# Opening of a two-layer encoder kernel: x brought in twice, once with its columns as rows, and two weight tiles of the mixer rounded later

## What is computed

```
x = layer_norm(ALPHA * x + 0.5 * (silu(x @ w_up[:, :2816]) * (x @ w_up[:, 2816:])) @ w_down)   # ffn1
u, q, k, v, qi, ki, wi, g_ssm, g_attn = split(x @ w_in)
y_ssm  = state_space(u); y_attn = sparse_attention(q, k, v, qi, ki, wi, rel_bias)
merged = sigmoid(g_ssm) * (y_ssm @ w_branch[0]) + sigmoid(g_attn) * (y_attn @ w_branch[1])
x = layer_norm(ALPHA * x + merged @ w_out)                                                       # mixer
x = layer_norm(ALPHA * x + 0.5 * swiglu(x, ffn2_w_up) @ ffn2_w_down)                             # ffn2
```

## Time and profile before

| what | us |
|---|---|
| median of 3 runs (lowest, highest) | 1124.35 (1123.41, 1125.34) |
| the profiled execution | 1129.07 |
| its span, first to last instruction | 1127.0 |
| PE busy in it | 1114.4 (99%) |
| PEld busy | 923.8 (82%) |
| DVE busy | 754.8 (67%) |
| ACT busy | 559.9 (50%) |
| POOL busy | 400.7 (36%) |

### The profile page before, as it was taken

One profiled execution on the slowest core, in us unless ns is written; L12 is line 12 of the kernel. 1 busy time (PEld: TensorE's weight loads), 2 busy tenths in 40 slices (PEclk: granted clock), 3 DMA queues, 4 the chain that ended last, 5 costly groups with the idle time before them and its releaser, 6 DMA issues.

```text
span 1127.0 us, 17832 instructions
## 1 busy us (share of the span) xinstructions
PE 1114.4 (99%) x6019; PEld 923.8 (82%) x6019; DVE 754.8 (67%) x1086; ACT 559.9 (50%) x807; POOL 400.7 (36%) x567
## 2 busy tenths in 40 slices
PE   9999999999999999999999999999999999999997
PEld 7888888898788888888888888889876888888886
DVE  5656745789977865775575555477895787555544
ACT  5545443574783554544344545336737735454440
POOL 2789986107700288997600000011374000000001
PEclk9999999999999999999999999999998999999999
DMA  8865653644565586565367575536544566757541
GB/s 268 257 203 187 219 187 107 207 142 148 155 208 203 173 235 204 184 224 183 116 207 221 168 242 187 192 95 206 164 134 128 192 206 205 223 162 248 188 149 38
DMA packets 158865, 207.51 MB, mean 184 GB/s; under 512 B 13161, under 2 KB 107689, under 8 KB 158801
## 3 DMA queue, kind: packets, MB, share of 16 engines
q1 hardware_dynamic: 155216, 201.77, 55.8%
q10 hardware_dynamic: 2560, 3.30, 1.2%
q0 software_dynamic: 1024, 1.61, 0.8%
HBM read 205.56 MB, written 1.06 MB: 183 GB/s over the span
## 4 chain that ended last, share of the span: by engine, by line
PE 86%; DVE 7%; issue 3%; DMA 2%; ACT 1%; SPq 0%; POOLq 0%; POOL 0%; DVEq 0%; ACTq 0%
PE ps L736 26%; PE ps L738 26%; PE ps L737 26%; DVE wlo L1257 3%; PE ps L763 2%; DMA raw<-in_w_in 2%; DVE score L1450 1%; PE ps L753 1%; PE ps L994 1%; PE ps L1067 1%; DVE gates L1422 1%; PE ps L1131 1%; PE ps L1133 1%; PE ps L1134 1%; ACT whi L422 0%
## 5 line engine op out<-in xcount | busy, mean ns | idle before, releaser
L1257 DVE TENSOR_TENSOR wlo<-raw,whi 128x1024 fp32r<-128x1024 f32 (+1 forms) x372 | 477.2, 1301 | 190.4 <-ACT whi L422 177.4
L422 ACT CAST whi<-raw 128x1024 fp32r<-128x1024 f32 (+1 forms) x372 | 385.2, 1044 | 292.4 <-PE ps L738 221.2
L736 PE MATMUL ps<-whi,xh 128*128 128x512 f32 x988 | 390.5, 395 | 0.0
L738 PE MATMUL ps<-whi,xl 128*128 128x512 f32 x988 | 383.3, 388 | 0.0
L737 PE MATMUL ps<-wlo,xh 128*128 128x512 f32 x988 | 382.9, 388 | 0.0
L736 PEld LDWEIGHTS ps<-whi,xh 128*128 128x128 f32 x988 | 186.2, 188 | 40.1 <-issue 3.8
L738 PEld LDWEIGHTS ps<-whi,xl 128*128 128x128 f32 x988 | 186.0, 188 | 38.6
L737 PEld LDWEIGHTS ps<-wlo,xh 128*128 128x128 f32 x988 | 186.4, 189 | 35.3
L1666 POOL TENSOR_TENSOR rstd<-var_eps,cst 128x1 f32<-128x1 f32 x12 | 18.2, 1518 | 528.3 <-DVE var_eps L1304 519.2
L736 PE MATMUL ps<-whi,hh 128*128 128x512 f32 (+1 forms) x355 | 140.2, 395 | 0.0
L738 PE MATMUL ps<-whi,hl 128*128 128x512 f32 (+1 forms) x355 | 137.8, 388 | 0.0
(11 more groups left out here) (203 smaller groups left out, 1219.8 us busy)
## 6 DMA issues: line engine op xcount, KB each, us to landing
raw<-in_ffn_w_up SPq DMA_DIRECT2D x352, 256.0 KB, 4.0
raw<-in_ffn_w_down SPq DMA_DIRECT2D x176, 256.0 KB, 3.0
raw<-in_w_in SPq DMA_DIRECT2D x128, 256.0 KB, 3.5
raw<-in_w_branch SPq DMA_DIRECT2D x32, 256.0 KB, 3.1
raw<-in_w_out SPq DMA_DIRECT2D x32, 256.0 KB, 3.6
bias_g<-bias_rows ACTq DMA_DIRECT2D x16, 192.0 KB, 4.0
raw<-in_w_in SPq DMA_DIRECT2D x16, 148.0 KB, 2.2
affine<-in_ln_g SPq DMA_DIRECT2D x4, 512.0 KB, 5.3
```

The lines of the kernel that those rows point to most:

```text
L422: nc.scalar.copy(whi[:, s % RING, 0:w], raw[:, s % RAW, 0:w]).then_inc(S["hi_done"], 1)
L736: nc.tensor.matmul(o, ah, bh, start=start, stop=False)
L738: return nc.tensor.matmul(o, al, bh, start=False, stop=stop)
L1257: nc.vector.tensor_tensor(wlo[:, s % RING, 0:w], raw[:, s % RAW, 0:w], f32(whi[:, s % RING, 0:w]), ALU.subtract).then_inc(S["split_done"], 1)
```

## The change

The host passes x a second time as `x_t`, with columns as rows, in the same four quarters of 256 KB. SP loads these quarters into `x_cols`, ACT rounds them straight from there and DVE makes the remainders, without PE or PSUM. The 16 transposes of the opening are gone; x itself is loaded whole behind the loads of chunk 2. The first weight tile is loaded by one DMA of 256 KB and two of 128 KB, and it is rounded and split in two halves. The loads of identity, buckets, bias table and parity go to SP behind tile 3. The products of the opening are in a new order, with the bias table behind the last product of the first token tile; `warm_up` runs 19 times at one go, where it ran 7 and 4 times around four transposes. ACT rounds three more tiles (3 to 5) ahead of `store_bias`, and 6 and 7 behind it. In the mixer, tile 24 is rounded at j = 8 instead of j = 5, and tile 25 at j = 9 instead of j = 8.

```diff
-GATE_TILES = {1: 22, 2: 23, 5: 24, 8: 25, 12: 26, 13: 27, ...
+GATE_TILES = {1: 22, 2: 23, 8: 24, 9: 25, 12: 26, 13: 27, ...
...
+            def load_columns(i, half):
+                sp.dma_start(x_cols[:, i, half, :], A["x_t"][i, half]).then_inc(xt_landed[2 * i + half], 16)
+            def load_first(w):
+                dst = raw[:, 0, :].rearrange("p (t g n) -> p t g n", t=2, g=2)
+                sp.dma_start(dst[:, 0], w[0, :, 0, :, 0, :]).then_inc(S["first_landed"], 16)
+                for g in range(2):
+                    sp.dma_start(dst[:, 1, g], w[0, :, 1, g, 0, :]).then_inc(raw_landed[0], 16)
...
-                        load_x(0, 0)
-                        up_chunk(l, 0, s0, w_up, 0, range(2))
-                        load_x(1, 0)
-                        load_x(0, 1)
+                        load_columns(0, 0)
+                        load_first(w_up)
+                        load_columns(1, 0)
+                        up_chunk(l, 0, s0, w_up, 0, range(1, 2))
+                        load_columns(0, 1)
                         up_chunk(l, 0, s0, w_up, 0, range(2, 3))
-                        load_x(1, 1)
+                        load_columns(1, 1)
                         up_chunk(l, 0, s0, w_up, 0, range(3, 4))
-                        sp.dma_start(parity[:, :], A["parity"]).then_inc(S["parity_landed"], 16)
+                        load_consts()
                     else:
                         up_chunk(l, 0, s0 + 4 * c, w_up, c)
+                if n == 0:
+                    for i in range(NT):
+                        sp.dma_start(x[:, i, :], A["x"][0, tok(i), :]).then_inc(x_landed[i], 16)
...
-            x_hi(0, 0, [0])
-            splits(0, 2)
-            x_hi(0, 1, [0])
-            splits(2, 1)
-            x_hi(0, 0, [1])
-            splits(3, 1)
-            x_hi(0, 1, [1])
-            splits(4, 4)
-            store_bias()
+            columns_hi(0, 0)
+            act.wait_ge(S["first_landed"], 16)
+            nc.scalar.copy(whi[:, 0, 0:512], raw[:, 0, 0:512]).then_inc(S["first_hi"], 1)
+            act.wait_ge(raw_landed[0], 32)
+            nc.scalar.copy(whi[:, 0, 512:1024], raw[:, 0, 512:1024]).then_inc(S["hi_done"], 1)
+            columns_hi(1, 0)
+            splits(1, 1)
+            columns_hi(0, 1)
+            splits(2, 1)
+            columns_hi(1, 1)
+            splits(3, 3)
+            store_bias()
+            splits(6, 2)
...
             def opening(prep):
+                pe.wait_ge(S["xh_done"], part(0, 0, 0))
+                pe.wait_ge(S["first_hi"], 1)
+                product(xh, whi, 0, 0, 0, start=True)
...
+                for q in range(1, 4):
+                    for t in range(NT):
                         pe.wait_ge(S["x_ready"], part(0, t, q // 2))
+                        if t == 0:
+                            pe.wait_ge(S["hi_done"], q + 1)
+                        for k in (2 * q, 2 * q + 1):
+                            for a in (xh, xl):
+                                product(a, whi, q, k, t)
+                        if t == 0:
+                            wait_split(q)
+                        for k in (2 * q, 2 * q + 1):
+                            ins = product(xh, wlo, q, k, t, stop=k == KT - 1)
...
+                        elif q == 3:
+                            ins.then_inc(S["up_done"], 1)
+                            bias_table()
+                pe.wait_ge(S["ident_landed"], 16)
...
             pe.wait_ge(S["const_ready"], 1)
-            warm_up(7)
-            pe.wait_ge(S["ident_landed"], 16)
-            x_transpose(0, 0, [0])
-            warm_up(4)
+            warm_up(19)
```

More of the change, by code:

```diff
@@ L297, in wait_acc, with xt_part, x_cols_half @@
             eng.wait_ge(S["acc_done"], 3 * n + 2 * t + half + 1)
+    def xt_part(stage, i, half):
+        return part(stage, i, half) - 2 * NT
+    def x_cols_half(i, half):
+        return x_cols[:, i, half, :].rearrange("p (k n) -> p k n", n=P)
     def xt_half(i, half):
@@ L429, in x_hi @@
                 for half in halves:
-                    act.wait_ge(S["xt_done"], part(t, i, half))
+                    act.wait_ge(S["xt_done"], xt_part(t, i, half))
                     nc.scalar.copy(xh[:, 4 * half:4 * half + 4, tok(i)], xt_half(i, half)
@@ L747, in x_transpose @@
                 for half in halves:
-                    if stage == 0:
-                        pe.wait_ge(x_landed[2 * i + half], 16)
-                    else:
-                        pe.wait_ge(S["tok_ready"], ready(stage, i, half))
+                    pe.wait_ge(S["tok_ready"], ready(stage, i, half))
                     for k in range(4 * half, 4 * half + 4):
@@ new lines, in opening @@
+                product(xh, wlo, 0, 1, 0)
+                pe.wait_ge(S["xh_done"], part(0, 1, 0))
+                for k in range(2):
+                    product(xh, whi, 0, k, 1, start=k == 0)
+                    product(xh, wlo, 0, k, 1)
+                pe.wait_ge(S["x_ready"], part(0, 1, 0))
+                for k in range(2):
+                    ins = product(xl, whi, 0, k, 1)
+                ins.then_inc(S["pe_used"], 1)
+                for q in range(1, 4):
+                    for t in range(NT):
+                        pe.wait_ge(S["x_ready"], part(0, t, q // 2))
+                        if t == 0:
[7 more added lines that the diff above has]
+                            ins = product(xh, wlo, q, k, t, stop=k == KT - 1)
+                        if t == 1:
+                            ins.then_inc(S["pe_used"], 1)
+                        elif q == 3:
+                            ins.then_inc(S["up_done"], 1)
+                            bias_table()
@@ L1294, in norm @@
             def norm(n, s_end, i, aff, between=None):
+                if n == 0:
+                    dve.wait_ge(x_landed[i], 16)
                 for j in range(2):
@@ L1607, in _, with columns_lo @@
             nc.vector.memset(k0_t[:, 2:4, :], 0.0).then_inc(S["const_ready"], 1)
+            def columns_lo(i, half):
+                k = slice(4 * half, 4 * half + 4)
+                dve.wait_ge(S["xh_done"], part(0, i, half))
+                nc.vector.tensor_tensor(xl[:, k, tok(i)], x_cols_half(i, half), f32(xh[:, k, tok(i)]), ALU.subtract
+                                        ).then_inc(S["x_ready"], 1)
+            columns_lo(0, 0)
+            dve.wait_ge(S["first_hi"], 1)
+            nc.vector.tensor_tensor(wlo[:, 0, 0:512], raw[:, 0, 0:512], f32(whi[:, 0, 0:512]), ALU.subtract
+                                    ).then_inc(S["first_lo"], 1)
+            dve.wait_ge(S["hi_done"], 1)
+            nc.vector.tensor_tensor(wlo[:, 0, 512:1024], raw[:, 0, 512:1024], f32(whi[:, 0, 512:1024]), ALU.subtract
+                                    ).then_inc(S["split_done"], 1)
+            columns_lo(1, 0)
+            splits(1, 1)
+            columns_lo(0, 1)
+            splits(2, 1)
+            columns_lo(1, 1)
+            splits(3, 5)
             dve.wait_ge(S["ident_landed"], 16)
             nc.vector.tensor_copy(ident_bf[:, :], ident[:, :]).then_inc(S["const_ready"], 1)
[L1610 to L1617 removed]
             dve.wait_ge(S["const_ready"], 3)
```

72 lines of the change are left out of this document (28 added, 44 removed).

## The result

| | median us | lowest to highest | runs |
|---|---|---|---|
| before | 1124.45 | 1123.41 to 1126.14 | 16 |
| after | 1127.06 | 1125.68 to 1128.29 | 16 |

The ratio after to before is 1.0022, 95% interval 1.0015 to 1.0028: the change made the kernel 2.6 us slower. The forecast was 1122.4 with a range up to 1125.8, so both its value and its sign are wrong.

A forecast was written before the change was run, and what follows sets the result against it. PE, busy 99% of the span, was taken as the bound. Against the median, opening -0.8, first layer's mixer +0.7 and second layer's -1.8 made -1.9, so 1122.4 us (chance 0.40), range 1119.4 to 1125.8.

The forecast's parts named there:

- The opening's result: Opening: PE starts chunk 1 at 20.3 instead of 21.11, a gain of 0.8 us.
- Warm-up was to end at 8.35: Opening: 38 warm-up records, slow until about 7.0, then twice as fast, keep PE until 8.35, 1.2 us past today's first product.
- Tile 3, the one that I had: Opening: tile 3 lands at 12.2 and is ready at 14.5; PE wants it at 16.6, covered by 2 us.
- 323 GB/s: Opening: the load rate assumed, by which 3.15 MB up to tile 3 take 9.75 us from about 2.4.
- x's loads: SP's queue ahead of tile 12: 1.05 MB more, at most 3.25 us of loading, price 0 to 0.55 us, taken as 0.
- the cover of the tile behind x in the queue, tile 12: Chunk 1's second silu on ACT and what follows: 3.5 us of cover, 2.7 with PE 0.8 earlier.
- a gap at PE's transposes near 31: Sign of being wrong: PE waits at its transposes near 31 or 43 us because of x's loads.
- The waits moved to pair 1: Both mixers: no wait for ACT at pair 0's values, one of 0.7 to 1.5 us at pair 1's.
- The size of the gain, 1.8 us: Second layer's mixer, usual run without the clock's drop: pair 1's values at 853.6 instead of 855.4, 1.8 us gained.
- Rival (2): Mixer: tile 24 lands in time in timed runs, so the second layer loses 0.95 us; sum +0.85, 1125.2 us; chance 0.30.
- Rival (3): Opening: slow warm-up records hold PE, opening loses 0.55 us; 1126.8 us; decides from warm-up ending after 9.2; chance 0.08.
- +0.7 - 1.8 (mixer): Mixer: 0.7 us lost in the first layer at pair 1's values, 1.8 us gained in the second.

The follow-up runs named there:

- f1: The changed kernel, with no further edit, profiled a second time: 1127.71 us in one execution.
- e6: The kernel before, with chunk 0's second silu, the parameter columns and their DVE followers moved ahead of the rounding of tiles 8 to 11: 1124.19 us, ratio to before 1.0001.
- e7: The changed kernel with silu, columns and their DVE followers ahead of tiles 8 to 11, and tiles 24 and 25 back at j = 5 and 8: 1123.48 us.
- e8: The changed kernel with the whole loads of x moved behind the loads of the last chunk: 1124.73 us, ratio to before 0.9997.
- e0: The kernel before, unchanged, profiled a second time: 1126.13 us in one execution.
- e1: The changed kernel with the casts of tiles 24 and 25 put back to j = 5 and j = 8: 1126.73 us, ratio to before 1.0019.
- e2: The kernel before with only the casts of tiles 24 and 25 moved to j = 8 and j = 9: 1125.63 us, ratio to before 1.0008.
- e3: The changed kernel with chunk 0's second silu, the parameter columns and their DVE followers moved ahead of the rounding of tiles 8 to 11: 1124.10 us, ratio to before 0.9996.
- e10: The e7 kernel with 13 warm-up calls instead of 19: 1123.86 us, ratio to before 0.9992.
- e9: The changed kernel with the loads of identity, buckets and bias table issued by ACT at the start, as before: 1125.58 us, ratio to before 1.0004.
- f3: The kernel before with two more products at the head of POOL's parameter work in the first layer: 1129.61 us, ratio to before 1.0046.

## Why the prediction was wrong

**The opening's result held, in part by luck.** Warm-up was to end at 8.35 and ended at 7.67 (after) and 7.07 (f1); over the eleven traces with 19 calls the first product starts at 6.92 to 8.41, a spread from run to run such as the prediction expected. The sum let the records run slowly until 7.0. In after the step comes before 6 us (windows 4 to 6 and 6 to 7.1 us, columns as in the earlier trace rows):

```profile
4.00:6.00 2.00, 2.00 (x12) 2.00 (x12) 1.03 (x2) 1.00 (x3) 2.00 (x5) 1.00 0.92 262
6.00:7.10 1.10, 1.10 (x13) 1.10 (x12) 0.98 (x2) 0.43 (x1) 0.54 (x1) 1.00 1.00 285
```

Twelve records touch the first 2 us, thirteen the 1.1 us behind them. The clock column says 1.00 for both windows, so the trace doesn't show the step as one of the granted clock, only in the pace of the records. The bias table cost 0.95 in full, as sized (17.74 to 18.69). The 48 products took 11.6 us and not 11.0. So chunk 1 was to start at 20.3 and did at 20.21, since a warm-up that was 0.7 too long in the sum and products that were 0.6 too short offset each other. And in f1, 0.6 us earlier out of warm-up, it starts at 21.13, since PE waits for tile 1, whose landing I had not worked out:

```profile
11.33 0.47 PE L836 MATMUL ps<-whi,xh 128*128 128x512 f32 x1 [1.28 <-ACT whi L447]
```

Tile 3, the one that I had, was to land at 12.2, and in after its cast ended a wait for it at 14.17. 323 GB/s was a figure of a 2 us stretch, not of the whole opening. The kernel before has the same spread (21.11 and 22.23), so a difference of 0.9 to 1.1 us holds pair by pair. Over all traces chunk 1 starts at 21.43 on average in the five with the old opening and at 20.69 in the eleven with the new one and 19 calls, 0.7 us apart, and e6 against e7 gives 0.7 in the timed runs.

**The step that failed first: x's loads "between 0 and 0.55; I take 0, since the queue is not full".** The price was not 0: e8, without these loads there, is 2.3 us faster. I counted the cover of the tile behind x in the queue, tile 12, and of what waits for that. I did not look at the tile ahead of it. Tile 11 was in flight when x was issued at 24.91, and its transit went from 4.06 to 5.10 and 6.13 us. And I did not list what stands behind tile 11's cast on ACT: the second silu and the columns. The rows were there to ask for; in before the same cast has already a wait for its load, and only 0.4 us are spare, since `h` comes 2.69 us behind this cast, at 31.76, and PE is there at 32.12:

```profile
29.07 1.05 ACT L422 CAST whi<-raw 128x1024 fp32r<-128x1024 f32 x1 [0.72 <-DMA raw<-in_ffn_w_up]
```

So even with x at no cost, of the 0.8 us of the first profile only 0.4 could have passed this point: an earlier PE needs an earlier `h`, and tile 11 hangs on four slots of `raw`, not on PE. The change left tile 7's cast about where it was (21.65 and, in f1, 22.28, against 21.73 and 21.70) and delayed tile 11's behind it. The prediction did name "a gap at PE's transposes near 31 [...] because of x's loads" as a sign that it would be wrong; it gave it no price above 0.55.

**The step that was not made: POOL.** The edge at 143 us was 1.5 us wide in before. POOL's 110 us without a break start from ACT's copy at 30.30, which hangs on the same tile. POOL at 36% of the span looked harmless. But from 35 to 140 us it was busy for 95.1 of 105 us in before, and a result that is wanted at one time has a margin, whatever its engine's share. Each us by which tile 11 is late beyond that margin is lost for good, as f1 shows. This is the larger part of how 0.8 us of gain became a loss of 2.6; the 0.1 us at 32.21 in the first profile shows little of it.

**The mixer.** The waits moved to pair 1 as predicted, in both layers. The size of the gain, 1.8 us, is the second term that failed, and it was taken from one execution: I gave the usual run a gain of 1.8 us in the second layer by taking away only the clock's dip, and leaving the gap of 3.48 us. e0 has 1.14 us there. With this the two layers are alike, each trades a wait of 0.9 to 1.1 us at pair 0 for one of 0.9 at pair 1 behind an additional cast, and after against e1, e2 against before and e3 against e7 give a net loss of 0.3 to 0.9. Rival (2) had this mechanism, with 1.65 for both layers, too much; its 1125.2 lacked POOL. Rival (3), slow warm-up records, was to decide from a warm-up that ends later than 9.2; no trace has that, and in e10 a shorter one gains nothing.

**In sum.** Predicted were -0.8 (opening), +0.7 - 1.8 (mixer) and 0 (x), together -1.9. The timed medians, taken step by step, give: before to e6 -0.3 (the reordering alone), e6 to e7 -0.7 (opening), e7 to e3 +0.6 (mixer), e3 to after +3.0 (what hung on tile 11), together +2.6. The steps form a chain, so that their sum must be the measured difference; it is no check of them, and each is uncertain by some tenths, since the median of before differs by up to 0.3 between the batches. Of the 3.0, the place of x's loads accounts for 2.3 (e8); e9 shows that the place of the constants may have a share that can't be told apart.

## What to carry to other kernels

Before a load is added to a queue, list what is in flight at that moment, not only what comes behind, and for each tile list everything queued behind its first consumer. Small work that feeds an engine with a long chain (here one copy and one minimum for 110 us of POOL) belongs ahead of any instruction that waits for a load. And a gain at the start of a kernel must be followed to the first point at which its engine waits for another: what it gains is no more than the slack there, and the margin of every long side chain must be read from the trace, not from shares of busy time.

## What the runs showed of the hardware

**POOL's instructions have no fixed length.** The same chain took 109.66 us in before and 114.59 in e6, which starts it at 26.66. The rows by line of POOL's first 116 us, the 51 smallest operations, in before, in after and in f3:

```profile
L1642 POOL TENSOR_TENSOR small<-small 128x16 f32<-128x16 f32 x51 | 14.6, 286 | 3.9
```
```profile
L1694 POOL TENSOR_TENSOR small<-small 128x16 f32<-128x16 f32 x51 | 19.9, 390 | 3.9
```
```profile
L1642 POOL TENSOR_TENSOR small<-small 128x16 f32<-128x16 f32 x51 | 27.4, 538 | 3.9
```

Each row has the same instructions on the same shapes, 286 to 538 ns on average. Another row of the same shape, `small<-small,cst` x31, goes the other way (532 ns in before, 371 in f3), so a row's mean says little of the whole chain (109.66 in before, 110.74 in f3). What sets the length of one instruction can be seen where the two engines stand side by side, here DVE and then POOL in after, 96 to 102 us:

```profile
97.62 5.30 DVE L1295 TENSOR_TENSOR wlo<-raw,whi 128x1024 fp32r<-128x1024 f32 x4 [1.42 <-ACT whi L447]
```
```profile
96.50 1.11 POOL L1694 TENSOR_TENSOR small<-small 128x16 f32<-128x16 f32 x4
97.69 3.95 POOL L1694 TENSOR_TENSOR small<-small,cst 128x16 f32<-128x16 f32 x3
```

Four small instructions ahead of `wlo` take 1.11 us together, the next three take 3.95, one for each remainder of DVE. It is so throughout: of the 867 records of `small<-small` in this stretch of the 17 traces, the 660 that meet no `wlo<-raw,whi` took 214 to 228 ns. 166 took over 300 ns, up to 1308; each of them began while such an instruction of DVE ran (one of them 4 ns ahead of it), and all ended 63 to 85 ns after it had ended. So a POOL instruction that starts beside this one of DVE is held until it is over, and the chain's length depends on how many it meets. The Trainium skill (GPSIMD Engine Reference, Specifications) says that the interface to SBUF is shared with VectorE, with contention when DVE's instruction has two inputs in SBUF, as `wlo<-raw,whi` has; the traces agree. No run took DVE's work away.

**The clock.** In the first profile of before the granted clock fell to its lower level behind a 3.48 us gap of PE. In the other profiles of before and after PE's waits reach 1.14 us in the mixers, in f3 1.63 us at the parameters, and the digits there stay at 9.
